# A chunked state recurrence in a two-block network: two chunks stacked on the 128 partitions, and the transposed inverse made by transposes

## The reference

```python
def _wkv7_step(state, inp):
    r_t, w_t, k_t, v_t, a_t, b_t = inp
    sa = jnp.einsum('bhvk,bhk->bhv', state, a_t)
    state = (state * w_t[:, :, None, :] + sa[..., None] * b_t[:, :, None, :]
             + v_t[..., None] * k_t[:, :, None, :])
    y = jnp.einsum('bhvk,bhk->bhv', state, r_t)
    return state, y
```

## Time and the profile before

| what | value |
|---|---|
| median of three runs | 2312.39 us |
| the profiled execution, first to last instruction (span) | 2300.0 us |
| span below the median of the runs by | 12.4 us |
| mean granted TensorE clock over the span | 0.965 |
| PE busy | 2098.2 us (91%) |
| state recurrence, 878.6 to 1111.3 us | 232.7 us |

### The profile page before, as it was taken

How to read it: one execution, slowest core, us unless ns; L and a number is a source line. 1 busy time by engine, 2 the same in 40 slices (tenths; PEclk the granted TensorE clock), 3 DMA queues, 4 the chain that set the end, 5 groups by cost and what they waited for, 6 DMA issues and landing times. The chain is left out here.

```text
span 2300.0 us, 37004 instructions
## 1 busy us (share of the span) xinstructions
PE 2098.2 (91%) x16054; PEld 1604.0 (70%) x16054; DVE 1301.8 (57%) x1837; ACT 775.1 (34%) x1119; POOL 268.3 (12%) x204
## 2 busy tenths in 40 slices
PE   7998989999979956888899999999958999999998
PEld 3885867887858716878466888886525666888885
DVE  2335756666454586555447676634395447676534
ACT  3434654444223350000224222322335634222322
POOL 0000003334400031111320000000005300000000
PEclk9997999999989988999989999999988999999999
DMA  7232002212313200000111333332310022333331
GB/s 281 92 101 75 1 10 80 67 56 73 101 55 113 79 18 3 4 4 4 37 55 64 92 101 94 99 92 80 99 62 1 1 74 64 93 100 95 98 93 45
DMA packets 47042, 158.63 MB, mean 69 GB/s; under 512 B 5328, under 2 KB 7504, under 8 KB 46880
## 3 DMA queue, kind: packets, MB, share of 16 engines
q1 hardware_dynamic: 45296, 151.84, 20.7%
q10 hardware_dynamic: 1584, 4.43, 0.6%
HBM read 154.10 MB, written 2.14 MB: 68 GB/s over the span
## 5 line engine op out<-in xcount | busy, mean ns | idle before, releaser
L947 PE MATMUL banks<-up_x_high,up_w_high 128*128 128x512 f32 x1056 | 412.2, 390 | 8.5 <-DVE up_w_low L941 3.9
L948 PE MATMUL banks<-up_x_low,up_w_high 128*128 128x512 f32 x1056 | 411.6, 390 | 0.0
L949 PE MATMUL banks<-up_x_high,up_w_low 128*128 128x512 f32 x1056 | 411.5, 390 | 0.0
L941 DVE TENSOR_TENSOR up_w_low<-weight_ring,up_w_high 128x1024 fp32r<-128x1024 f32 x132 | 161.6, 1226 | 269.4 <-ACT up_w_high L936 269.4
L936 ACT CAST up_w_high<-weight_ring 128x1024 fp32r<-128x1024 f32 x132 | 138.3, 1049 | 365.3 <-PE banks L949 340.7
L947 PEld LDWEIGHTS banks<-up_x_high,up_w_high 128*128 128x128 f32 x1056 | 198.5, 188 | 53.7 <-issue 11.6
L949 PEld LDWEIGHTS banks<-up_x_high,up_w_low 128*128 128x128 f32 x1056 | 198.6, 188 | 41.5
L948 PEld LDWEIGHTS banks<-up_x_low,up_w_high 128*128 128x128 f32 x1056 | 198.6, 188 | 40.9
L1483 POOL TENSOR_TENSOR hproj_w_low<-weight_ring,hproj_w_high 128x1024 fp32r<-128x1024 f32 x43 | 106.0, 2466 | 505.6 <-ACT hproj_w_high L1283 505.6
L1002 DVE SCALAR_TENSOR_TENSOR act<-banks,cols,act 128x511 f32<-128x511 f32 (+1 forms) x176 | 131.8, 749 | 6.3
L1158 PE MATMUL banks<-hproj_x_high,hproj_w_high 128*128 128x512 f32 x224 | 90.0, 402 | 5.1 <-DVE hproj_x_low L1434 3.4
(11 more groups left out here) (474 smaller groups left out, 4241.0 us busy)
## 6 DMA issues: line engine op xcount, KB each, us to landing
weight_ring<-in_up SPq DMA_DIRECT2D x88, 512.0 KB, 3.6
weight_ring<-in_down SPq DMA_DIRECT2D x44, 512.0 KB, 3.6
weight_ring<-in_w_ada SPq DMA_DIRECT2D x24, 512.0 KB, 5.6
weight_ring<-in_w_rkv SPq DMA_DIRECT2D x24, 512.0 KB, 3.3
weight_ring<-in_w_in SPq DMA_DIRECT2D x20, 512.0 KB, 3.4
weight_ring<-in_w_out SPq DMA_DIRECT2D x16, 512.0 KB, 3.3
weight_ring<-in_w_q SPq DMA_DIRECT2D x8, 512.0 KB, 4.5
weight_ring<-in_w_k SPq DMA_DIRECT2D x8, 512.0 KB, 3.4
```

The lines of the kernel that those rows point to most:

```text
L941: nc.vector.tensor_tensor(w_low[:, n % 2, :], ring[:, i % RING, :], w_high[:, n % 2, :].bitcast(f32), ALU.subtract).then_inc(wl_made, 1)
L947: nc.tensor.matmul(PS[:, bank, :], high, x_high[:, k, :], start=start, stop=False)
L948: nc.tensor.matmul(PS[:, bank, :], high, x_low[:, k, :], start=False, stop=False)
L949: return nc.tensor.matmul(PS[:, bank, :], low, x_high[:, k, :], start=False, stop=stop)
```

## The change

It restacks the operands of the recurrence so that more work goes into each TensorE instruction.

- Grams: the chunks of a pair get one partition half each. One matmul has at_ and rt together as 128 moving columns (act tiles become views of one tensor, and xx and xm exchange places so that a stride reaches both). The 64 rows of corrections and the 64 rows of values are stacked in one table for each chunk; the separate gram for G is gone, VectorE's start makes the first GT from the table.
- Turns: one 128x128 transpose per channel tile and pair, 3 x 8 in a pass. ScalarE copies v whole and kt and bt in two halves, which it puts so that b and k of one chunk stack on 128 partitions (keys; a spare tile serves the first pass).
- Inverse: G is updated as before. GT isn't updated by matmuls but turned from G by 4 transposes (t_level, one PSUM bank for both x), copied by ScalarE; the last level updates GT alone (last_level).
- make_w is split: make_ak (the values' part, into its own bank, ScalarE puts it into W_) and the state's part, which VectorE adds. GpSimd then copies the values over that part of the table, and u is written beside it by VectorE and ScalarE, a half each. make_y is then, per channel tile, two 64x64 matmuls on the state and two with 128 rows on the stack; make_s has 128 rows throughout.
- The order of a pass: w of the previous pair's first chunk comes after the second gram, u after the fourth, y after the turns, s in level 1 together with make_ak of the second chunk, whose w, u, y and s stand in levels 2 to 5.

```diff
-        r, kx, v, xx, xm, a_, sig, tmp = F[1:9]
+        r, kx, v, xm, xx, a_, sig, tmp = F[1:9]
...
+        both = sb("act", [P, 5, KT, T])
+        F = [both[:, i] for i in range(5)]
...
+        table = [(sig, tmp)[i // 2][:, i % 2 * 4:i % 2 * 4 + 4, :].rearrange("p a b -> p (a b)").rearrange("p (j t w) -> p j t w", j=2, t=8) for i in range(4)]
...
+        T_BANK, AK_BANK, LAST_BANK = 4, 5, (4, 5)
+        pair_of = lambda t, i: t[:, :, i * P:(i + 1) * P]
+        even_keys = lambda i: pair_of(kt, i)
+        odd_keys = lambda i: pair_of(bt, i - 1) if i else spare[:, :, :]
+        keys = lambda c: odd_keys(c // 2) if c % 2 else even_keys(c // 2)
...
+        def gram(i, x, e):
+            c = 2 * i + e
+            if i or x:
+                pe.wait_ge(gram_moved, 4 * i + 2 * x + e - 1)
             for p in range(8):
+                for t, half in ((bt, HALVES[1 - e]), (kt, HALVES[e])):
+                    dst = PS[half, 2 * e + p // 4, p % 4 * P:(p % 4 + 1) * P]
+                    mm = nc.tensor.matmul(dst, of_head(t, p, HALVES[x], c), at_and_rt(p, HALVES[x], c), start=True, stop=True)
             mm.then_inc(grams, 1)
+        def turn(i, n, t):
+            if i or n:
+                pe.wait_ge(turned_moved, (0, 1, 3)[n] + 5 * i)
+            if n == 0 and i:
...
+                mm = nc.tensor.transpose(PS[:, 4 + p // 4, p % 4 * P:(p % 4 + 1) * P], pair_of(t, i)[:, p, :], mat("ident"))
...
+        def start_level(i, x):
+            pe.wait_ge(start_made, 2 * i + x + 1)
+            if x == 0:
+                pe.wait_ge(turned_moved, 5 * i + 5)
+            else:
+                pe.wait_ge(t_moved, 10 * i + 1)
+            for m in range(4):
+                mm = nc.tensor.transpose(PS[:, T_BANK, m * P:(m + 1) * P], GT_[i % 2][x][:, m * P:(m + 1) * P], mat("ident"))
+            mm.then_inc(t_made, 1)
+        def q_level(i, l, x):
+            if l == 1:
+                pe.wait_ge(t_moved, 10 * i + x + 1)
+            else:
+                pe.wait_ge(g_moved, 8 * i + 2 * (l - 2) + x + 1)
+            for p in range(8):
+                for u in range(2):
+                    nt = table[(2 * i + 1 - u) % 4]
+                    mm = nc.tensor.matmul(PS[HALVES[p % 2], 2 * x + u, tile_cols(p // 2)], nt[HALVES[u], x, p, 0:LC], G_[x][HALVES[u], tile_cols(p)],
+                                          start=True, stop=True)
+            mm.then_inc(q_made, 1)
+        def g_level(i, l, x):
+            pe.wait_ge(q_moved, 10 * i + 2 * (l - 1) + x + 1)
+            if l > 1:
+                pe.wait_ge(t_moved, 10 * i + 2 * (l - 1) + x + 1)
+            for p in range(8):
+                for u in range(2):
+                    side, at0 = HALVES[p % 2], place(p // 2, u)
+                    mm = nc.tensor.matmul(PS[HALVES[u], 2 * x + p % 2, T // 2 + p // 2 * HD:T // 2 + (p // 2 + 1) * HD], GT_[i % 2][x][side, at0], Q_[x][side, at0],
+                                          start=True, stop=True)
+            mm.then_inc(g_made, 1)
+        def t_level(i, l, x):
+            pe.wait_ge(g_moved, 8 * i + 2 * (l - 1) + x + 1)
+            if x:
+                pe.wait_ge(t_moved, 10 * i + 2 * l + 1)
+            for m in range(4):
+                mm = nc.tensor.transpose(PS[:, T_BANK, m * P:(m + 1) * P], G_[x][:, m * P:(m + 1) * P], mat("ident"))
+            mm.then_inc(t_made, 1)
+        def last_level(i, x):
+            pe.wait_ge(q_moved, 10 * i + 9 + x)
+            pe.wait_ge(t_moved, 10 * i + 10)
+            if x:
+                pe.wait_ge(ak_moved, 2 * i)
+            for p in range(8):
+                for u in range(2):
+                    side, at0 = HALVES[p % 2], place(p // 2, u)
+                    mm = nc.tensor.matmul(PS[side, LAST_BANK[x], at0], Q_[x][side, at0], GT_[i % 2][x][side, at0], start=True, stop=True)
+            mm.then_inc(last_made, 1)
...
+        def make_ak(c):
+            half = HALVES[c % 2]
+            if c % 2:
+                pe.wait_ge(ak_moved, c)
+            else:
+                pe.wait_ge(last_moved, c + 2)
+            if c == 6:
+                pe.wait_ge(turned_moved, 20)
+            for p in range(8):
+                for x in range(2):
+                    mm = nc.tensor.matmul(PS[HALVES[p % 2], AK_BANK, x * (T // 2) + p // 2 * HD:x * (T // 2) + (p // 2 + 1) * HD],
+                                          table[c % 4][half, x, p, 0:LC], pair_of(v, c // 2)[half, p, x * HD:(x + 1) * HD], start=True, stop=True)
+            mm.then_inc(ak_made, 1)
...
+                    side, at0 = HALVES[p % 2], x * (T // 2) + p // 2 * HD
+                    mm = nc.tensor.matmul(PS[HALVES[1 - c % 2], 6 + p % 2, at0:at0 + HD], GT_[c // 2 % 2][x][side, place(p // 2, 1 - c % 2)],
+                                          W_[side, at0:at0 + HD], start=True, stop=True)
...
+            pe.wait_ge(u_moved_act, c + 1)
+            pe.wait_ge(u_moved_dve, c + 1)
+            pe.wait_ge(v_put, c + 1)
             for p in range(8):
                 for half in HALVES:
+                    nc.tensor.matmul(PS[half, 7, tile_cols(p)], S_[half, tile_cols(p)], of_head(rt, p, half, c), start=True, stop=False)
+                for x, half in enumerate(HALVES):
+                    mm = nc.tensor.matmul(PS[half, 7, tile_cols(p)], table[c % 4][:, x, p, 0:LC], table[c % 4][:, x, p, LC:P], start=False, stop=True)
             mm.then_inc(y_made, 1)
         def make_s(c):
             for p in range(8):
+                for x, half in enumerate(HALVES):
+                    mm = nc.tensor.matmul(PS[half, 6, tile_cols(p)], keys(c)[:, p, x * HD:(x + 1) * HD], table[c % 4][:, x, p, 0:LC], start=True, stop=True)
...
         for i in range(NCH // 2):
+            if i:
+                make_ak(2 * i - 2)
+            gram(i, 0, 0)
+            gram(i, 0, 1)
+            carry(i, 0)
+            turn(i, 0, v)
+            gram(i, 1, 0)
+            gram(i, 1, 1)
+            carry(i, 1)
+            turn(i, 1, kt)
+            turn(i, 2, bt)
+            carry(i, 2)
+            start_level(i, 0)
+            start_level(i, 1)
             for l in range(1, LEVELS + 1):
+                for x in range(2):
+                    q_level(i, l, x)
+                if l < LEVELS:
+                    for x in range(2):
+                        g_level(i, l, x)
+                    if l == 1 and i:
+                        make_ak(2 * i - 1)
+                    carry(i, 2 + l)
+                    for x in range(2):
+                        t_level(i, l, x)
+                else:
+                    carry(i, 7)
+                    for x in range(2):
+                        last_level(i, x)
+        make_ak(NCH - 2)
+        for step in range(8):
+            if step == 1:
+                make_ak(NCH - 1)
+            carry(NCH // 2, step)
...
+        def start(i, x):
+            if i:
+                dve.wait_ge(u_made, 2 * i - 2)
+            for q in range(2):
+                for u in range(2):
+                    dve.wait_ge(gram_moved, 4 * i + 2 * x + 2 - u)
+                    dst = by_row_half(GT_[i % 2][x])[HALVES[q], u]
+                    src = table[(2 * i + 1 - u) % 4][HALVES[u], x].rearrange("p (m q) w -> p m q w", q=2)[:, :, q, 0:LC]
+                    nc.vector.tensor_tensor(dst, src, over(first_mask_t[HALVES[u], :], 4), ALU.mult).then_inc(start_part, 1)
+            dve.wait_ge(start_part, 8 * i + 4 * x + 4)
+            nc.vector.tensor_tensor(by_pair(GT_[i % 2][x]), by_pair(GT_[i % 2][x]), over(ident64, 8), ALU.add).then_inc(start_made, 1)
...
+        def take_g(i, l, x):
+            dve.wait_ge(g_made, 8 * i + 2 * (l - 1) + x + 1)
+                dve.wait_ge(t_moved, 10 * i + x + 1)
+            else:
+                dve.wait_ge(t_made, 10 * i + 2 * (l - 1) + x + 1)
+                dve.wait_ge(g_moved, 8 * i + 2 * (l - 2) + x + 1)
+            nc.vector.tensor_tensor(by_row_half(G_[x]), g_bank(x), by_row_half(G_[x]), ALU.add).then_inc(g_moved, 1)
+        def take_last(i, x):
+            dve.wait_ge(last_made, 2 * i + x + 1)
+            dve.wait_ge(t_moved, 10 * i + 9 + x)
+            nc.vector.tensor_tensor(GT_[i % 2][x], PS[:, LAST_BANK[x], :], GT_[i % 2][x], ALU.add).then_inc(last_moved, 1)
...
+            nc.gpsimd.tensor_copy(table[c % 4][half, :, :, 0:LC], pair_of(v, c // 2)[half].rearrange("p t (x w) -> p x t w", x=2)).then_inc(v_put, 1)
...
+        def take_turned(i, n):
+            act.wait_ge(turned, 3 * i + n + 1)
+            src = lambda half: PS[half, 4:6, :].rearrange("p a (t w) -> p (a t) w", w=P)
+            low, high = HALVES
+            if n == 0:
+                nc.scalar.copy(pair_of(v, i), src(slice(0, P))).then_inc(turned_moved, 1)
+            elif n == 1:
+                nc.scalar.copy(even_keys(i)[low], src(low)).then_inc(turned_moved, 1)
+                nc.scalar.copy(odd_keys(i)[high], src(high)).then_inc(turned_moved, 1)
+            else:
```

(62 more changed lines are left out.)

262 lines of the change are left out of this document (77 added, 185 removed).

## The result

The changed kernel takes 2319.4 us (median of 18 runs, 2310.95 to 2325.52) against 2308.78 for the kernel before (18 runs, 2303.49 to 2317.84): ratio 1.0047, 95% interval 1.0037 to 1.0058. It is slower by about 10.6 us; I had forecast 2303 and a gain of 9.3.

The account below looks back on a forecast made before the run. Instruction supply to TensorE paced the recurrence stage, then the chain of waits. 41.4+3x53.0+20.0 = 220.4, plus 3 for bursts, 223.4 against 232.7: 9.3 us less, forecast 2303 us, range 2268 to 2336.

Parts of the forecast that it names:

- A: Rival: array shape changes in the recurrence are mostly hidden, giving 28 us back, 2276 us; chance 0.22.
- B: Rival: each array shape change in the recurrence costs 0.32 us, 32 us more in all, 2335 us; chance 0.14.
- C: Rival: TensorE's clock falls, a quarter of the stage at 1.2 GHz, some 36 us more, 2339 us; chance 0.06.
- Records and packets: TensorE's instructions in the recurrence stage: 7616 records become 4832, 59.5 packets become 37.8, so supply stops being the bound.
- 3.83 us a packet: Supply pace of TensorE's 128-record instruction packets in the stage; alone it would let the changed stage end in 145 us.
- 3 us added for bursts: Added to the stage's 220.4 us because bursts, such as level 5's 160 records in 4.2 us, still run into supply.
- Change of shape at 0.15 us: Alternating matmul shapes on TensorE: about 190 changes at 0.15 us, 28 us in all; 16 in each y.
- Levels: Inverse levels: 5.1 us without carry; in a full pass 6.8, 5.3, 5.7, 8.8 and 4.2, sum 30.8 us.
- A full pass 53.0: One full pass of the recurrence: front part 22.1 plus levels 30.8 us, 53.0 against 58.0 before.
- wait of 2.3 us for ScalarE: In a full pass's front part, TensorE waits 2.3 us after the turn of k for ScalarE's two half copies.
- First pass 41.4, tail 20.0: Ends of the recurrence stage: first pass 41.4 us against 42.3 before, tail 20.0 against 16.3.
- The granted clock: TensorE in the recurrence stage: granted clock 1.00 in the passes, as no scheduled gap is above 2.3 us.

Follow-up runs that it names:

- e8: Kernel before the change, with the q products of each pair's second chunk issued twice (640 records more): ratio 1.0085.
- e3: Changed kernel with y's products on the state issued first and those on the stack behind them, instead of alternating: ratio 0.9970.
- e1: Changed kernel with 16 unread matmuls (32 records) filling TensorE's wait between the turns of k and b: ratio 1.0027.
- e11: Kernel of e6 with the second chunk half's transposes in their own PSUM bank, so they needn't wait for ScalarE's copy: ratio 0.9806, 2260.2 us.
- e9: Changed kernel with 32 filling records in each pass's wait and 10 unread records ahead of the stage, nothing else: ratio 1.0001.
- e2: Changed kernel with the turn of b put into PSUM banks 0 and 1, so it needn't wait for ScalarE's copies of k: ratio 0.9979.
- e6: Kernel of e4 with the grams of the two row halves interleaved over four quadrants, PSUM banks by row half: ratio 0.9870.
- e4: Changed kernel with both y grouped in two blocks and b turned into PSUM banks 0 and 1: ratio 0.9924.

## Why the prediction was wrong

It ended on the wrong side: slower by 10.6 us where I had forecast a gain of 9.3. Both lie within the 11.6 us that I had set as no change, a case I gave 0.36. That 2319.4 us falls between 2268 and 2336 is luck: that width was made for A and B, which didn't happen, and left out C, which did. By its steps:

- **Records and packets.** Right: 4832 records, 38 packets (37.8), no regular gaps. That supply paced the kernel before fits e8's total of 17 to 20 us, but not two of its full passes (14 and 16 ns a record); the fixed 3.83 us a packet is refuted. Of the 3 us added for bursts the first two passes show 1.5, as single gaps.
- **Change of shape at 0.15 us.** Right: 0.147 in the trace, 0.143 from e3. Rival A (hidden) and B (0.32) fall. That a change costs as much as five records on two quadrants (29 ns) made y, at 16 a time, the dearest step: e3 won 0.77% with one loop cut in two, part of it through the clock.
- **Levels.** Right at full clock. The first pass has 5.7 (its first 2.5 us at half clock), 5.4, 5.75 (0.52 of it waiting for issue) and 5.0 us, with 5.1 forecast. The second pass of e1 has 6.9, 5.7, 5.7 and 8.8 (forecast 6.8, 5.3, 5.7 and 8.8); in the changed kernel the first of these is 7.5, with 2.2 us at half clock, and the last 9.5. e11 shows the named cause, t1 behind ScalarE's copy.
- **A full pass 53.0.** Right at full clock: 53.3, 53.7, 53.0 in e1. The wait of 2.3 us for ScalarE is there too: 2.13.
- **First pass 41.4, tail 20.0.** 42.0 in e9, with 3.4 us at half clock. The tail was never seen wholly at full clock; it was 25.4 with 17.7 us at half, 23.2 in e1 with 9.5. Carried on along these two it would be 20.6 without any, an estimate.
- **The granted clock.** This step failed. The sum took 2.4 GHz for the whole stage and put the fall of the clock aside as rival C at 0.06, "against: no gap in my schedule is above 2.3 us, and the passes before, with gaps up to 1.5, had 1.00". That argued from gaps up to 1.5 us to one of 2.3, and the schedule has exactly one such gap in a full pass. It was where the clock fell, three times out of three: e1 (filled) and e2 (removed) both keep 1.00 in the passes. The alternating y behind it had its part, for e3 keeps the wait and loses 0, 3.4 and 3.4 us to half clock instead of 13.7 each. In the first pass the grams at half clock didn't lift it as they did before. The excess over the forecast's stage, 252.4 less 223.4 = 29.0 us by the windows, is 12.2 in the first pass, 14.4 in the passes and 5.4 in the tail, less the 3 of supply. These are the profiled executions; by the medians the miss is 10.6 and 9.3, 19.9 us. C's own size was near: it had 36 us for a quarter of the schedule at half clock, and the 88 us less the 29.0 that they cost are 59 us of schedule, a quarter of it. 29.0 us over 88 less 2.8 is 0.34 us for each further us at half clock; e1 against the changed kernel gives 14.7 us for 45 fewer, 0.32.

By the Trainium skill, TensorE: Matmul & The Clock Gate, Part 4 (PE-mode transpose), transposes don't count as busy in the same way, which the prediction named in favour of C. The clock did fall behind eight transposes and a wait. But in e2 sixteen transposes stand in a row and the clock stays at 1.00, so the runs don't show that rule to be the cause.

What stays open: what exactly lowers and lifts the clock. It also fell where no wait of 2 us stands ahead: for 6.8 us in the grams of the second pass in e9 and in e3. In the changed kernel's tail it falls 7.5 us after the tail's start, with no wait above 0.8 us since then. In the first pass it took 2.8 us with the old grams, 5.9 with e6's four quadrants, 19.4 in e4 and 29.7 in the changed kernel, whose grams use one row half at a time, though TensorE was busy for 24.5 of those 29.7 us and had no wait at all in the first 17.9. e6 changed the quadrants and the waits together, so the two aren't told apart. Open too is a run with the tail at full clock; I didn't try to fill it.

## What to carry to other kernels

An edit that takes instructions from an engine with a gated clock makes it idle more, and a first wait of some 2 us can cost more than the instructions did: look for the longest wait in the new schedule and give it cover (here another bank for one result) before counting the gain. Look at what stands behind the wait as well, and at the granted clock of each stretch after the change, since one wait cost 13.7 us at half clock in one order of y and 3.4 or nothing in the other. Sort small matmuls by array shape; here each change cost about as much as five records. Cut records only as far as they bind, then look for the buffer that makes two half steps wait for each other.

## What the runs showed of the hardware that I had not expected

- 128-column fp32 matmuls on four 64x64 quadrants issue every 27 ns a record, on the two quadrants of one row half every 54.
- One wait of 2.13 us with an alternating y behind it brought 13.7 us at 1.2 GHz, in each of three passes; 32 filling records (1.7 us) in it removed all three. The same wait with y in two blocks behind it brought 0, 3.4 and 3.4 us (e3).
- 17.9 us without a wait, grams on one row half at a time and two turns, did not bring the clock back in the first pass; with ten records of 128x512 ahead of the stage (4.3 us) it was at 2.4 GHz when the stage began.
- From 64x64 to 128x64 and back it takes 0.20 us from the start of the last weight load to the next, whether or not the matmuls add to one address (e3).
- 640 further records of 15 ns issue cost 27 ns each over the stage of the kernel before (14 and 16 in two of its full passes), 18 ns each in e11.
